# State-space moves, norms and small products of a hybrid encoder layer rebuilt

## The reference

```
q = rmsnorm(q.reshape(b, l, SB_HEADS, SB_HEAD_DIM), q_norm_g)
k = rmsnorm(k.reshape(b, l, SB_HEADS, SB_HEAD_DIM), k_norm_g)
bu_re = jnp.einsum('blgh,gph->blgp', u, bbar_re)
bu_im = jnp.einsum('blgh,gph->blgp', u, bbar_im)
_, _, xr, xi = lax.associative_scan(combine, (ar, ai, bu_re, bu_im), axis=1)
y = (jnp.einsum('blgp,ghp->blgh', xr, c_re)
     - jnp.einsum('blgp,ghp->blgh', xi, c_im)
     + d_skip * u)
```

## Time and profile before

| | us |
|---|---|
| median of 3 runs | 713.35 (713.32 to 713.65) |
| the profiled execution, whole | 713.8 |
| its span, first to last instruction | 712.1 |
| TensorE busy | 703.3 |
| ScalarE, VectorE, GpSimd busy | 320.2, 413.0, 187.7 |

### The profile page before, as it was taken

One profiled execution on the slowest core, in us unless ns is written; L12 is line 12 of the kernel. 1 busy time (PEld: TensorE's weight loads), 2 busy tenths in 40 slices (PEclk: granted clock), 3 DMA queues, 4 the chain that ended last, 5 costly groups with the idle time before them and its releaser, 6 DMA issues.

```text
span 712.1 us, 13993 instructions
## 1 busy us (share of the span) xinstructions
PE 703.3 (99%) x5552; PEld 669.5 (94%) x5552; DVE 413.0 (58%) x557; ACT 320.2 (45%) x474; POOL 187.7 (26%) x215
## 2 busy tenths in 40 slices
PE   8999999999999999999999999999999999999998
PEld 7899899989999999999999999999999998888887
DVE  5763388868787746544766656666666662222221
ACT  4754343558788654334434434444334432211120
POOL 7899999940000022232010110101010110000000
PEclk9999999999999999999999999999999999999999
DMA  8173534546211233333333333233323343333331
GB/s 231 54 204 79 104 109 91 108 98 171 59 33 60 68 90 111 89 90 89 89 90 94 101 99 89 88 88 88 88 89 95 104 122 99 96 97 96 96 97 45
DMA packets 140520, 69.25 MB, mean 97 GB/s; under 512 B 24067, under 2 KB 138471, under 8 KB 140479
## 3 DMA queue, kind: packets, MB, share of 16 engines
q1 hardware_dynamic: 140319, 68.65, 35.1%
q10 hardware_dynamic: 160, 0.02, 0.0%
HBM read 63.19 MB, written 4.28 MB: 95 GB/s over the span
## 4 chain that ended last, share of the span: by engine, by line
PE 85%; ACT 4%; DVE 4%; SPq 3%; issue 1%; DMA 1%; POOL 0%; ACTq 0%; DVEq 0%
PE ps L1796 78%; SPq L524 1%; PE ps L2037 1%; ACT hi L904 1%; PE ps L1846 1%; PE ps L1979 1%; PE ps L2004 1%; DMA stack<-in_ssm_d_dram 1%; ACT xh L973 1%; SPq L661 1%; SPq L617 1%; SPq L626 1%; PE ps L1855 1%; PE ps L2021 0%; PE ps L2214 0%
## 5 line engine op out<-in xcount | busy, mean ns | idle before, releaser
L1288 DVE TENSOR_TENSOR lo<-raw,hi 128x1024 fp32r<-128x1024 f32 (+2 forms) x102 | 135.2, 1325 | 155.0 <-ACT hi L904 154.7
L1796 PE MATMUL ps<-xh,hi 128*128 128x264 f32 (+2 forms) x1088 | 220.0, 283 | 0.1
L904 ACT ACTIVATE hi<-raw 128x1024 fp32r<-128x1024 f32 (+2 forms) x102 | 111.5, 1094 | 239.8 <-PE ps L1796 233.1
L1796 PE MATMUL ps<-xl,hi 128*128 128x264 f32 (+2 forms) x1088 | 218.9, 282 | 0.0
L1796 PE MATMUL ps<-xh,lo 128*128 128x264 f32 (+2 forms) x1088 | 218.4, 282 | 0.0
L1796 PEld LDWEIGHTS ps<-xh,hi 128*128 128x128 f32 x1088 | 167.3, 189 | 1.7 <-issue 0.8
L1796 PEld LDWEIGHTS ps<-xl,hi 128*128 128x128 f32 x1088 | 166.7, 188 | 0.0
L1796 PEld LDWEIGHTS ps<-xh,lo 128*128 128x128 f32 x1088 | 166.4, 188 | 0.0
L887 POOL TENSOR_TENSOR cv<-cv 128x512 f32<-128x512 f32 x22 | 28.3, 1286 | 226.7 <-DVE cv L1748 226.7
L1796 PE MATMUL ps<-ah,hi 128*128 128x512 f32 (+1 forms) x198 | 73.8, 373 | 0.0
L1796 PE MATMUL ps<-ah,lo 128*128 128x512 f32 (+1 forms) x198 | 73.2, 370 | 0.0
(11 more groups left out here) (291 smaller groups left out, 965.6 us busy)
## 6 DMA issues: line engine op xcount, KB each, us to landing
raw<-in_w_up_dram SPq DMA_DIRECT2D x88, 256.0 KB, 3.1
raw<-in_w_in_dram SPq DMA_DIRECT2D x52, 256.0 KB, 3.3
raw<-in_w_down_dram SPq DMA_DIRECT2D x16, 384.0 KB, 3.4
raw<-in_w_down_dram SPq DMA_DIRECT2D x16, 320.0 KB, 3.9
raw<-in_w_o_dram SPq DMA_DIRECT2D x16, 256.0 KB, 2.9
xtok<-in_x_dram SPq DMA_DIRECT2D x4, 512.0 KB, 5.5
raw<-in_w_ssm_proj_dram SPq DMA_DIRECT2D x8, 256.0 KB, 2.9
out_dram<-yt SPq DMA_DIRECT2D x7, 256.0 KB, 2.4
```

The lines of the kernel that those rows point to most:

```text
L904: act.activation(hi[slot][:, 0:n * P], raw[slot][:, 0:n * P], ACT.Copy)\
L1288: dve.tensor_tensor(lo[slot][:, 0:n * P], raw[slot][:, 0:n * P], hi[slot][:, 0:n * P].bitcast(F32), ALU.subtract)\
L1796: ins = pe.matmul(o, weights[w], acts(a, c), start=start and i == 0, stop=stop and i == 2)
```

## The change

- **Taps.** `bpair` is 32 columns wide instead of 48 and the products of the four group pairs of a round go to four tiles of 32 columns of the PE array, into one stretch of 128 columns; ACT copies 128x128 (before, two copies of 16x512). They wait for both parts of the output maps, and DVE now makes one part in every round (units 6, 7, 8 and 12), POOL the other.
- **Toeplitz matrix.** Each round's taps are written to a DRAM array whose rows have 112 zeros ahead of them (written once, `no_taps`), and one DMA reads all eight lags from overlapping rows.
- **Inputs** are read once, in 8 DMAs for all rounds, after the last write; `uc` holds all four rounds. `y_write` is one DMA a round, `y_read` eight.
- **Norms.** `sel` is 32 columns wide and each of the four sums has a tile of the array of its own; the sums, not the rates, go to DRAM, come back as 128x33, get their rates there (`rates`, unit 10), and are written and read for every row.
- **Readout.** The products of `hout` and `xst` are cut into two halves of 64 output rows, so that they use four tiles of 64x64.
- **Values** are turned in three steps (2, 4 and 4 tiles) in bank 7, after the `prep` of rounds 1, 2 and 3. **Scores**: the masks stand ahead of the region products of their bank.

```diff
-         5: [("square", 0)], 6: [("square", 1)],
-         7: [("square", 2)], 8: [("square", 3), ("prep", 0)], 9: [("state", 0), ("norms", 0)],
-         10: [("prep", 1), ("out_map", 2)], 11: [("readout", 0), ("state", 1)],
-         12: [("prep", 2), ("turn_v", 0), ("out_map", 3)] + [("scale", i) for i in range(4)], 13: [("readout", 1), ("state", 2)],
-         14: [("prep", 3), ("turn_v", 1)], 15: [("readout", 2), ("state", 3)],
+         5: [("square", 0)], 6: [("square", 1), ("out_map", 0)],
+         7: [("square", 2), ("out_map", 1)], 8: [("square", 3), ("out_map", 2), ("prep", 0)],
+         9: [("state", 0), ("norms", 0)],
+         10: [("prep", 1), ("turn_v", 0), ("rates", 0)], 11: [("readout", 0), ("state", 1)],
+         12: [("prep", 2), ("turn_v", 1), ("out_map", 3)] + [("scale", i) for i in range(4)], 13: [("readout", 1), ("state", 2)],
+         14: [("prep", 3), ("turn_v", 2)], 15: [("readout", 2), ("state", 3)],
...
-MOVES = {2: [("u_write", 0)], 3: [("u_write", 1)], 4: [("u_write", 2), ("u_read", 0)],
-         5: [("u_write", 3), ("u_read", 1)],
-         7: [("rms_write", 0)], 8: [("rms_read", 0)], 9: [("toep", 0)],
-         11: [("norm_write", 0)],
-         12: [("norm_read", 0), ("u_read", 2), ("toep", 1), ("y_write", 0)],
-         14: [("u_read", 3), ("toep", 2), ("y_write", 1)],
+MOVES = {2: [("u_write", 0)], 3: [("u_write", 1), ("no_taps", 0)], 4: [("u_write", 2)],
+         5: [("u_write", 3), ("u_read", 0)],
+         7: [("rms_write", 0)], 8: [("rms_read", 0)], 9: [("norm_write", 0), ("toep", 0)],
+         10: [("norm_read", 0)], 11: [("rate_write", 0), ("rate_read", 0)],
+         12: [("toep", 1), ("y_write", 0)],
+         14: [("toep", 2), ("y_write", 1)],
...
-NORM_ROWS = (0, 32)
-TURN_BANK = (4, 4)
+NORM_TILE = 32
+TURN_BANK = 7
...
+        def lagged(r):
+            rows = taps_dram[r]
+            return bass.AP(rows.tensor, rows.offset, [[GH, T8], [TAPS, GH * 2 * RP], [1, P]])
...
+            def u_read(_):
+                for u in u_out:
+                    sp.wait_ge(u, 16)
+                src = u_dram.rearrange("(r g h) j c -> j h (r g) c", h=GH, r=ROUNDS)
                 for j in range(T8):
                     p0 = GH * (T8 - 1 - j)
-                    sp.dma_start(uc[p0:p0 + GH, r % 2], src[j]).then_inc(u_in[r], 16)
+                    sp.dma_start(uc[p0:p0 + GH].rearrange("p r g c -> p (r g) c"), src[j])\
+                        .then_inc(u_in, 16)
...
+            def no_taps(_):
+                sp.wait_ge(masks_set, 3)
+                sp.dma_start(taps_dram[:, :, :, 0:LAGS].rearrange("r h g t -> (h g) r t"),
+                             xst[:].rearrange("p c i n -> p (c i n)")[:, 0:ROUNDS * LAGS]
+                             .rearrange("p (r t) -> p r t", t=LAGS)).then_inc(no_taps_out, 16)
             def toep_move(r):
-                move_taps(sp, r)
+                sp.wait_ge(kern_set, r + 1)
+                sp.dma_start(taps_dram[r, :, :, LAGS:TAPS].rearrange("h g t -> g h t"), kern[:])\
+                    .then_inc(kern_out[r], 16)
+                if r:
+                    sp.wait_ge(y_ps, r)
+                else:
+                    sp.wait_ge(no_taps_out, 16)
+                sp.wait_ge(kern_out[r], 16)
+                sp.dma_start(toep[:], lagged(r)).then_inc(toep_in[r], 16)
             def y_write(r):
                 sp.wait_ge(yg_set, r + 1)
-                dst = y_dram[r * P:(r + 1) * P].rearrange("(g h) j c -> j h g c", h=GH)
-                for j in range(T8):
-                    sp.dma_start(dst[j], yg[GH * j:GH * (j + 1)]).then_inc(y_out[r], 16)
+                sp.dma_start(y_dram[r].rearrange("j h g c -> (j h) (g c)"),
+                             yg[:].rearrange("p g c -> p (g c)")).then_inc(y_out[r], 16)
             def y_read(_):
                 for r in range(ROUNDS):
-                    sp.wait_ge(y_out[r], 16 * T8)
+                    sp.wait_ge(y_out[r], 16)
                 sp.wait_ge(st_set, ROUNDS)
                 sp.wait_ge(y_ps, ROUNDS)
-                sp.dma_start(yT[:], y_dram.rearrange("(r p) j c -> p r j c", p=P)).then_inc(y_in, 16)
+                for g in range(2 * RP):
+                    sp.dma_start(yT[GH * g:GH * (g + 1)].rearrange("p r j c -> p (r j) c"),
+                                 y_dram[:, :, :, g].rearrange("r j h c -> h (r j) c"))\
+                        .then_inc(y_in, 16)
...
             def norm_write(_):
+                sp.wait_ge(ss_v, 1)
+                for i in range(4):
+                    row = NORM_TILE * i
+                    sp.dma_start(sum_dram[:, 3 - i], row_v[row:row + 2, :]).then_inc(sum_out, 16)
+            def norm_read(_):
+                sp.wait_ge(sum_out, 64)
+                sp.dma_start(nrm[:, 0], sum_dram.rearrange("h i c -> (h i c)")
+                             .rearrange("(p c) -> p c", c=NORM_COLS)).then_inc(sum_in, 16)
+            def rate_write(_):
                 sp.wait_ge(rows_set, 1)
-                for n, row in enumerate(NORM_ROWS):
-                    sp.dma_start(norm_dram[4 * n:4 * n + 4].rearrange("r b c -> r (b c)"),
-                                 row_r[row:row + 4, :]).then_inc(norm_out, 16)
...
+            def rate_read(_):
+                sp.wait_ge(rate_out, 16)
+                for h in range(2):
+                    sp.dma_start(sq_all[h * DH:(h + 1) * DH], rate_dram[h].partition_broadcast(DH))\
+                        .then_inc(rate_in, 16)
+            move = {"norm_write": norm_write, "norm_read": norm_read,
...
-            output_map(0, (0, 1))
+            output_map(0)
             pool.tensor_copy(decay[:, :, 1:NC], sm[:, S_D2, :].unsqueeze(2)
                              .broadcast_to([P, PAIRS, NC - 1])).then_inc(decay_set, 1)
-            output_map(1, (0, 1))
+            output_map(1)
             input_map(1)
-            output_map(2, (1,))
+            output_map(2)
             input_map(2)
-            output_map(3, (1,))
+            output_map(3)
             input_map(3)
...
+            def rates(_):
+                act.wait_ge(sum_in, 16)
+                link(act.activation(nrm[:, 1], nrm[:, 0], ACT.Ln))
+                act.activation(nrm[:, 1], nrm[:, 1], ACT.Exp, scale=-0.5).then_inc(rs_a, 1)
...
                 if r >= HOUTS:
                     dve.wait_ge(y_ps, r - HOUTS + 1)
+                if r == 0:
+                    dve.wait_ge(pw_set, 1)
+                    for u in u_out:
+                        dve.wait_ge(u, 16)
...
                 pe.wait_ge(sq_ready, 4)
-                rows = slice(0, NORM_ROWS[1] + 4)
                 for c in range(2):
                     for i in range(4):
-                        w = HL if norm_of(i)[0] else HLL
-                        ins = pe.matmul(ps[rows, 6 + c, 0:w], sel[:, i], sq[i][:, c * w:(c + 1) * w],
-                                        start=i == 0, stop=i == 3, skip_group_check=True)
+                        c0 = c * (HL if norm_of(i)[0] else HLL)
+                        ins = pe.matmul(ps[NORM_TILE * i:NORM_TILE * (i + 1), 6 + c, 0:HL],
+                                        sel[:, i], sq[i][:, c0:c0 + HL],
+                                        start=True, stop=True)
...
                 pe.wait_ge(h_pool, r + 1)
-                if r >= 2:
-                    pe.wait_ge(h_dve, r - 1)
-                for i in range(RP):
-                    for c in range(2):
-                        ins = pe.matmul(ps[0:3 * GH, 6, i * P:(i + 1) * P],
-                                        bpair[:, c, r * RP + i, :],
-                                        hout[r % HOUTS][:, c, i, 0:T8, :].rearrange("p i h -> p (i h)"),
+                pe.wait_ge(h_dve, r + 1)
+                for c in range(2):
+                    for i in range(RP):
+                        rows = slice(2 * GH * i, 2 * GH * (i + 1))
+                        ins = pe.matmul(ps[rows, 6, 0:P], bpair[:, c, r * RP + i, :],
+                                        hout[r % HOUTS][:, c, i, 0:T8, :]
+                                        .rearrange("p i h -> p (i h)"),
                                         start=c == 0, stop=c == 1)
                 ins.then_inc(k_ps, 1)
...
+                pe.wait_ge(toep_in[r], 16)
                 pe.wait_ge(st_set, r + 1)
                 for g in range(2 * RP):
                     for half in range(2):
                         part = slice(ST * half, ST * half + ST)
-                        pe.matmul(group_out(g)[part], toep[:, g, part], uc[:, r % 2, g, :],
+                        pe.matmul(group_out(g)[part], toep[:, g, part], uc[:, r, g, :],
                                   start=g < 2, stop=False, skip_group_check=True)
                 for c in range(2):
                     for g in range(2 * RP):
                         part = slice(ST * (g % 2), ST * (g % 2) + ST)
-                        ins = pe.matmul(group_out(g), hout[r % HOUTS][part, c, g // 2, 1:T8 + 1, :]
```

(16 more changed lines are left out.)

209 lines of the change are left out of this document (96 added, 113 removed).

## The result

The changed kernel takes 718.67 us (median of 7 runs, 717.56 to 722.31) against 713.44 (713.32 to 714.06): a ratio of 1.0072, 95% interval 1.0053 to 1.0092. **It is slower by 5.2 us**; forecast was 705.3 with a range to 710.8. The profiled execution of after is one of the long ones: 722.1 us in all, 3.4 over the median, with a span of 720.4. Its mean granted clock (the share of full speed at which TensorE was let run) is 0.987; the seven runs lie between 0.987 and 0.993, and before was at 1.000. Its sums are made against the span of 712.1 of before. Of the experiments further down, one run of e7 (750.8) and one of e9 (1368.4) stand far outside their fellows and are left out.

A forecast was written before the change was run, and what follows sets the result against it. TensorE's own stream was taken as the bound, busy 703.3 of 712.1 us. Taps 5.4 + norms 2.5 + readout 1.6 - waits 1.5 = 8.0 us gained, so 705.3 for the median, range 702.0 to 710.8.

The forecast's parts named there:

- What bounds the kernel: Whole kernel: the time is TensorE's own stream, busy 703.3 of 712.1 us; other engines' savings count only through waits.
- Taps: Taps products on four tiles of 32 columns at once: 1.3 us less in each of four rounds, 5.4 us.
- Norms: Norm sums, each of the four on a tile of its own: 2.5 us less.
- Readout: Readout products on four quadrants, 0.085 us a record on its tile: 0.4 us less each, 1.6 for four.
- Rivals 1, 2 and 3: Only two tiles at once, 713.4, 6%; quadrants not paying, 710.7, 6%; readout paced at about 25 ns, 706.9, 18%.
- Edits at nothing: Value transposes, moved mask products, VectorE's added output map parts and the inputs read in one go: taken as 0 us.
- Wait (a): First readout, for the last value tiles behind ScalarE's and VectorE's share of unit 10: 0.5 us, between 0 and 2.
- rival 4: SP's queue is held by the taps' landing and matrix read, so weights come late and TensorE starves: 715.4, 7%.
- Wait (b) and (c): Waits of 1.5 us at the third readout for VectorE's turned values, and 0.7 at the last readout for the scan.
- The direction: Whole kernel: faster by more than 0.2% (1.4 us) 87%, within it 6%, slower by more 7%.

The follow-up runs named there:

- e7: e4, and VectorE makes its part of every output map, as in the changed kernel: 716.18 us, 1.0031 of before.
- e9: e6 with ten products that nobody reads on TensorE ahead of the second readout's wait for the Toeplitz matrix: 708.30 us, 0.9926 of before.
- e1: The changed kernel with the inputs read round by round again, after units 4, 5, 12 and 14: 717.05 us, 1.0043 of before.
- e6: e5, and the inputs read round by round after units 4, 5, 6 and 7: 712.51 us, 0.9976 of before.
- e10: e6 with the rates read behind the matrix of round 1 instead of ahead of its taps: 709.44 us, 0.9946 of before.
- e8: The changed kernel, reading only two of the Toeplitz matrix's eight lags (128 KB instead of 512 KB a round): 716.15 us, 1.0040 of before.
- e5: The changed kernel with taps written one step earlier and the matrix read behind the next weights: 715.33 us, 1.0032 of before.
- e2: The changed kernel with the values turned as before, after the products of rounds 2 and 3: 720.57 us, 1.0098 of before.
- e3: The changed kernel with the matrix read in 8 reads of 64 KB, one for each lag: 720.96 us, 1.0100 of before.
- e17: The kernel before with a long TensorE pause, for 24 GpSimd memsets, ahead of the fourth head's scores: 721.06 us, 1.0100 of before.
- e18: e17 with its pause filled by eight products that nobody reads: 718.66 us, 1.0068 of before.
- e15: e10 with GpSimd's eight products of the GLU's input started only when the last scan is done: 706.83 us, 0.9900 of before.
- e4: The kernel before with only the norms on four tiles and the readout on quadrants: 714.88 us, 1.0027 of before.
- e16: The kernel before with GpSimd's eight products of the GLU's input started only when the last scan is done: 716.64 us, 1.0049 of before.

## Why the prediction was wrong, step by step

- **What bounds the kernel.** Right: an edit gains what it takes from TensorE's stream and costs what it makes TensorE wait. The gains were 11.1, the forecast's 9.5; the waits grew by 12.2, the forecast's by 1.5.
- **Taps.** Right: 1.31 for 1.3 a round.
- **Norms.** Right: 2.58 shorter as a block and 2.4 in the path, for 2.5.
- **Readout.** The sign was right, the forecast half of what came: 0.4 each for a measured 0.83. I took 0.085 as the cost of a record on its tile; 64 records last 1.17, so (1.17 - 0.26)/63 gives a step of 14 ns, 0.06 on each of four tiles, which is the end of my range with the largest gain. Rivals 1, 2 and 3 fall with it. The Trainium skill ("TensorE: Matmul & The Clock Gate", section "Wait — 56ns, not 53.3ns?") has about 25 ns as the least step; for records that alternate between four tiles the measurement decides against it.
- **"Edits at nothing": the inputs.** Wrong. I wrote that they are read in one go two units earlier than they are needed, and asked only whether the inputs would be there in time. What mattered is what is issued behind them: the weights of unit 8, which landed in 7.70. Of the 5.9 us lost up to `prep(0)` 4.2 are theirs (a wait of 2.4, low clock 1.8); e1, e6 and e10 have this place at 75.1 to 75.3.
- **Wait (a).** This is the step that failed at the first readout: a wait of 0.5 was taken, and 4.04 came. The chain was right up to the issue of the weights: 7.8 from the start of the norm products by my lowest terms, 7.4 measured (90.02 to 97.45). (The 95.1 that I gave for its end is the lowest sum of its terms; their upper ends give 96.6.) But I took 3.3 for the landing from the earlier trace rows, a median of weights that stand behind other weights, and behind 512 KB it was 7.98. ScalarE's high part came at 105.46 instead of 95: 5.6 of that is the delay that after has brought along (the start and unit 8), and 4.7 the landing. e8 (less data) gives back 2 of 4 us, e5 (other order) all of it; e2 excludes the values, and e3 leaves open what the form of the read does.
- **The matrix by way of DRAM, rival 4.** It was the nearest to what happened: a hold at SP and at the landing, with 715.4. Its place was named, its condition too (11.5 us for the two transfers; at the second readout they took 16), but I gave it 7% since by the 2.3 of the earlier trace rows the two took 4.6. That row is of 64 KB each and with nothing large ahead. The bound should have been made from the amount that stands ahead on the queues: the rates alone are some 1.06 MB, and it took e10 to show it.
- **Wait (b) and (c).** The third readout waited 2.9 (1.5 taken, 0 to 3 named). The cause named, VectorE's chain, is right; that it was slowed by GpSimd's products was not in the working, although before had it too: its two xst operations last 1.90 at 137.03, beside those products, and 0.77 at 153.29, behind them. The last readout waited 1.1 (0.7 taken), but the number was near by luck: VectorE's scan had ended at 162.07, and TensorE waited until 163.39 for the matrix.
- **The low clock.** Missing altogether. I priced a wait at its length; 5.7 us of after's profiled execution are low clock behind waits. e17 and e18 measure such a stretch, and e9 shows it in the changed kernel.
- **The direction.** Faster was given 87%. Three of the four causes (weights behind inputs, weights behind the matrix, rates ahead of the taps) are one: a queue was read as a list of instructions with a time of issuing, and not as bytes ahead of the next weights. With that put right in e15, and GpSimd's products moved, the forecast's 705.3 stands against 706.8 measured; that the two are so near is in part luck, since the readouts gained 1.7 more than forecast and e15's waits lie at places that the forecast does not name.

What stays open: why some runs of e6 keep the full clock and others of the same kernel don't; how much of e4's and e7's loss is low clock; and whether one read with 8 outermost is slow by its form.

## What to carry to other kernels

When small transfers are merged into large ones, ask what is issued behind them on the same queue, and price that by the bytes ahead of it, not by its usual landing time. Put a large transfer behind the next urgent one, and issue the first half of a round trip through memory a step earlier, so that nobody waits for the landing. In a kernel whose TensorE is busy 99% of the time, a wait can cost more than its length, since the clock falls behind it (1.6 times for one of 4.6 us here, hardly more than its length for one of 1.3); and time taken out of TensorE's stream is worth only what the engines that feed it have in slack.

## What the runs showed of the hardware

- 64 products of 64x64 tiles with 66 columns, on four quadrants, go at a step of 14 ns (records; 1.17 us in all), 128x64 ones on two tiles at 31.
- A wait of 1.3 us cost 1.5, one of 4.6 cost 7.6; behind the latter the granted clock is 0.50 at 225 to 230 us and 1.00 at 230 to 235. Filled with useless products, it cost 5.2. Ten such products made e9 4 us faster than e6.
- Weights of 256 KB that land in 3.3 us (the median of before) land in 5.8 behind a read of 128 KB (e8) and in 8.0 behind one of 512 KB (after). In e3, where the 512 KB go out in eight reads over 6.4 us, they land in 3.4. Eight transfers of 132 KB in pieces of 264 bytes take 6.4 each; the same in 32 of 33 KB take 1.9 each, but 0.5 us each of SP's time.
- VectorE's operations with both operands in SBUF are slow beside GpSimd's 128x528 products (1.5 to 1.7 us each): a 128x528 one takes 1.7 us for 0.71, and two of 128x260 take 2.91 for 0.77. Those with one operand in PSUM are not: in e10, with GpSimd's products at 131.60 to 143.26, two operations on PSUM and SBUF take 0.70 and 0.69 from 137.74 on, and the next, on SBUF alone, takes 1.49 for its usual 0.43. The Trainium skill ("SBUF — State Buffer", section "SBUF: two separate sides") says that a VectorE operation with two SBUF inputs and a GpSimd one share a pair of ports, and that whichever starts first holds it for its whole instruction; after, e15 and e16 agree.
